# Two fp32r parts instead of three bf16 parts for the rows that the experts gather

## What is computed

```python
xn = rms_norm(x, norm_moe)                       # 256 x 1024
logits = xn @ w_router + b_router
top_val, top_idx = lax.top_k(logits, 4)          # 4 of 32 experts for a token
gates = softmax(top_val)
# for every expert e, with the tokens `tok` that chose it:
hact = clamped_swiglu(xn[tok] @ w_gate_up[e] + b_gate_up[e])   # 1024 -> 2 x 1024 -> 1024
out[tok] += gate * (hact @ w_down[e] + b_down[e])              # 1024 -> 1024
```

## Time and profile before

| | |
|---|---|
| median of 3 runs | 1271.41 us |
| the profiled execution's own time | 1271.19 us |
| its span, first to last instruction | 1269.2 us |
| TensorE (PE) busy | 1187.5 us, 94% of the span |
| VectorE (DVE) busy | 481.7 us, 38% |
| ScalarE (ACT) busy | 250.1 us, 20% |
| mean granted TensorE clock | 0.995 of 2.4 GHz |
| read from device memory | 459.76 MB, 363 GB/s over the span |

### The profile page before, as it was taken

How to read it: one execution, slowest core, us unless ns; L and a number is a source line. 1 busy time by engine, 2 the same in 40 slices (tenths; PEclk the granted TensorE clock), 3 DMA queues, 4 the chain that set the end, 5 groups by cost and what they waited for, 6 DMA issues and landing times.

```text
span 1269.2 us, 18417 instructions
## 1 busy us (share of the span) xinstructions
PE 1187.5 (94%) x7495; PEld 611.8 (48%) x7495; DVE 481.7 (38%) x744; ACT 250.1 (20%) x353; POOL 5.4 (0%) x11
## 2 busy tenths in 40 slices
PE   8999999999799999999999899999999898999996
PEld 7999998998533333333333333333333333333332
DVE  6867867664422322222223222222222222222224
ACT  6338544534410100001000000001000000000002
POOL 0000100000000000000000000000000000000000
PEclk9999999999899999999999999999999999999999
DMA  8525645534999999999999999999999999999995
GB/s 326 195 100 200 253 153 210 186 136 179 400 404 428 428 429 427 428 429 429 429 428 429 427 428 429 429 429 428 429 429 427 429 429 429 428 429 428 428 427 230
DMA packets 36688, 461.28 MB, mean 363 GB/s; under 512 B 4256, under 2 KB 4400, under 8 KB 5552
## 3 DMA queue, kind: packets, MB, share of 16 engines
q1 hardware_dynamic: 36144, 460.16, 86.9%
q0 software_dynamic: 224, 0.54, 0.1%
q10 hardware_dynamic: 288, 0.12, 0.0%
HBM read 459.76 MB, written 1.05 MB: 363 GB/s over the span
## 4 chain that ended last, share of the span: by engine, by line
PE 50%; DMA 47%; ACT 1%; DVE 1%; issue 1%; SPq 0%; DVEq 0%; ACTq 0%
DMA late<-in_w_gate_up 44%; PE ps L1275 21%; PE ps L1146 5%; PE ps L1147 5%; PE ps L1148 5%; DMA raw<-in_w_down 3%; PE ps L1166 2%; PE ps L1165 2%; PE ps L1167 2%; PE ps L1181 2%; PE ps L1326 2%; PE ps L1300 1%; PE ps L1334 1%; DMA raw<-in_dense 1%; PE ps L1234 1%
## 5 line engine op out<-in xcount | busy, mean ns | idle before, releaser
L1275 PE MATMUL ps<-late,s 128*64 128x512 f32 x1128 | 515.9, 600 | 58.0 <-DMA late<-in_w_gate_up 57.0
L1276 PE MATMUL ps<-late,s 128*64 128x512 f32 x1128 | 516.0, 600 | 0.0
L1275 PEld LDWEIGHTS ps<-late,s 128*64 128x64 f32 x1128 | 143.9, 137 | 383.7 <-issue 260.6
L1033 DVE TENSOR_TENSOR res<-res,ps 128x1024 f32<-128x1024 f32 x66 | 80.6, 1221 | 247.7 <-PE ps L1326 247.7
L1146 PE MATMUL ps<-act_hi,whi 128*128 128x256 f32 x576 | 164.1, 285 | 3.8 <-DVE act_lo L693 1.7
L1147 PE MATMUL ps<-act_lo,whi 128*128 128x256 f32 x576 | 163.1, 283 | 0.0
L1148 PE MATMUL ps<-act_hi,wlo 128*128 128x256 f32 x576 | 163.1, 283 | 0.0
L609 ACT ACTIVATE s<-ps 128x512 f32<-128x512 f32 x64 | 34.7, 595 | 561.1 <-PE ps L1276 561.1
L1276 PEld LDWEIGHTS ps<-late,s 128*64 128x64 f32 x1128 | 143.9, 137 | 0.0
L712 DVE TENSOR_TENSOR wlo<-raw,whi 128x2048 fp32r<-128x2048 f32 x47 | 107.4, 2289 | 51.8 <-ACT whi L442 51.7
L1275 PE MATMUL ps<-raw,s 128*64 128x512 f32 x272 | 123.9, 598 | 0.5 <-DMA raw<-in_w_down 0.3
(11 more groups left out here) (178 smaller groups left out, 967.3 us busy)
## 6 DMA issues: line engine op xcount, KB each, us to landing
late<-in_w_gate_up SPq DMA_DIRECT2D x125, 2048.0 KB, 25.5
raw<-in_w_down SPq DMA_DIRECT2D x32, 2048.0 KB, 25.6
raw<-in_dense SPq DMA_DIRECT2D x51, 1024.0 KB, 4.8
late<-in_w_down SPq DMA_DIRECT2D x16, 2048.0 KB, 25.3
s<-in_w_down SPq DMA_DIRECT2D x16, 2048.0 KB, 25.3
raw<-in_w_gate_up SPq DMA_DIRECT2D x2, 2048.0 KB, 9.7
s<-in_w_gate_up SPq DMA_DIRECT2D x1, 2048.0 KB, 12.3
res<-in_x SPq DMA_DIRECT2D x2, 512.0 KB, 4.0
```

The costliest lines, as they stand in the source:

```text
L1033: V.tensor_tensor(res[:, t, :], res[:, t, :], ps[:, OUT_BANK[t]:OUT_BANK[t] + 2, :].rearrange("p b n -> p (b n)"), ALU.add)\
L1275: nc.tensor.matmul(ps[0:SLOTS, bank, :], x_tile, lower, start=start, stop=stop)
L1276: return nc.tensor.matmul(ps[SLOTS:P, bank, :], x_tile, upper, start=start, stop=stop)
```

## The change

The rows are cut into two parts instead of three. ScalarE writes the leading part in fp32r (the rounded value), VectorE subtracts it from the row and writes the remainder in fp32r. `rest_rows_of` and `middle_rows` and their semaphores go; `low_rows` becomes the multiply-and-subtract that `rest_rows_of` was. [...] A gather has 8 x 2 x 2 = 32 products instead of 48. The two parts lie where the three lay (s2 and s3), the one-hot gets a tile of its own.

```diff
-        half = [s[:, :].bitcast(BF16) for s in (s2, s3)]
...
+        xpart = [nc.alloc_sbuf_tensor_at(f"xpart{i}", [P, TT * D], F32R, offset=at)[:, :].rearrange("p (t d) -> p t d", d=D)
+                 for i, at in enumerate((s2_at, s3_at))]
+        onehot = sb("onehot", [P, TT, SLOTS], F32R)
...
-            def middle_rows(t):
-                act.wait_ge(S["part_rest"], t + 1)
-                nc.scalar.activation(xpart[1][:, t, :], rest_rows[:, t, :], ACT.Copy).then_inc(S["part_mid"], 1)
...
-            middle_rows(0)
...
-            middle_rows(1)
...
-            def rest_rows_of(t):
+            def low_rows(t):
                 dve.wait_ge(S["part_hi"], t + 1)
                 dve.wait_ge(S["rstd_done"], t + 1)
-                V.scalar_tensor_tensor(rest_rows[:, t, :], res[:, t, :], rstd[:, 6 + t:7 + t], xpart[0][:, t, :],
-                                       ALU.mult, ALU.subtract).then_inc(S["part_rest"], 1)
-
-            def low_rows(t):
-                dve.wait_ge(S["part_mid"], t + 1)
-                V.tensor_tensor(xpart[2][:, t, :], rest_rows[:, t, :], xpart[1][:, t, :], ALU.subtract)\
+                V.scalar_tensor_tensor(xpart[1][:, t, :], res[:, t, :], rstd[:, 6 + t:7 + t],
+                                       xpart[0][:, t, :].bitcast(F32), ALU.mult, ALU.subtract)\
                     .then_inc(S["part_low"], 1)
...
-            rest_rows_of(0)
             evacuate("xnT", 3, copied(xn_f))
             low_rows(0)
...
-            rest_rows_of(1)
...
-                    for n in range(3):
+                    for n in range(2):
                         for t in range(TT):
                             last = nc.tensor.matmul(ps[:, 5, k * SLOTS:(k + 1) * SLOTS],
                                                     xpart[n][:, t, k * P:(k + 1) * P], onehot[:, t, :],
-                                                    start=n == 0 and t == 0, stop=n == 2 and t == TT - 1)
+                                                    start=n == 0 and t == 0, stop=n == 1 and t == TT - 1)
```

More of the change, by code:

```diff
@@ L176, in build @@
         plain = KT * T
-        s0, s2, s3, s7, s8, s9 = (sb(f"s{i}", [P, plain]) for i in (0, 2, 3, 7, 8, 9))
+        s0 = sb("s0", [P, plain])
+        s2_at = (nc.sbuf_base + 31) // 32 * 32
+        s2 = sb("s2", [P, plain])
+        s3_at = (nc.sbuf_base + 31) // 32 * 32
+        s3 = sb("s3", [P, plain])
+        s7, s8, s9 = (sb(f"s{i}", [P, plain]) for i in (7, 8, 9))
         s15 = sb("s15", [P, 2 * wide])
@@ L259, in build @@
             lam_abs lam_exp pads_zero xr_done pool_done decay_done inner_done mult_done scan_done
-            gelu_arg gelu_sig yb_done m_done lam_done rowmax prob_done part_hi part_rest part_mid part_low
+            gelu_arg gelu_sig yb_done m_done lam_done rowmax prob_done part_hi part_low
             rstd_done router_scaled gmat_zero gate_in gate_exp picked gmat_done bd_placed route_done
@@ L1338, in _ @@
             pe.wait_ge(S["part_hi"], TT)
-            pe.wait_ge(S["part_mid"], TT)
             pe.wait_ge(S["part_low"], TT)
```

## The result

The changed kernel takes **1308.44 us** (median of 4 runs, 1307.68 to 1309.77), the kernel before, run beside it, 1271.38 (4 runs, 1271.1 to 1272.06): a ratio of 1.0295, 95% interval 1.0283 to 1.0308. It is slower by 37 us; the time lies outside the range that was forecast. The profiled execution took 1307.78 us.

What follows compares the result with a forecast made beforehand. The prediction took the memory loads to bound the expert loop, with TensorE having slack. 0 in the loop, +0.8 us at its start and nothing at the end gave 1272.2 us, no change; range 1268.0 to 1278.0.

Steps and rivals of the forecast that it cites:

- the gather's cost: Gather in the loop: 32 products 111 ns apart take 3.44 us from first to last, 2.06 us more than now.
- the slack: Expert loop: TensorE waits 69.4 us in all for loads, so each of 31 gathers may grow by 2.24 us.
- 0 in the loop: Expert loop: the longer gathers, 64 us over 31, are hidden by the loads and add nothing.
- the thin products let the clock fall in every iteration: Rival, loop: 1.2 GHz after each gather costs a few us an expert, beyond the slack; chance 0.08 shared with two passes.
- The start: Before the expert loop: first gather starts about 1.5 us earlier but lasts 7.1 us; first release +0.8 us.
- the two bounds for the release: First buffer release at the loop's start: +2.9 us if the clock stays low throughout, -2.7 us if it never falls.
- The row between: Loop start: clock returns at 346.2, as expert 0 starts at 346.3; release at 350.0, +0.8 us.
- the first rival: Loop gather: products 120 ns apart make TensorE the bound, 3.1 us over the slack, 1275.3 us; chance 0.26.
- Two passes: Rival, loop gather: each product costs two passes, 63 distances, +104 us, about 1376; chance 0.08 shared with the falling clock.
- The faster start: Rival, loop start: the clock does not fall, first release 2.7 us sooner, 1268.7 us; chance 0.16.

Runs made afterwards that it cites:

- e1_split: The changed kernel with each gather of the loop cut into two halves of 16 products, the second behind the first two `down` chunks; 1274.62 us, ratio 1.0028.
- e2_long_bf16: The kernel before with 72 more bf16 products in each gather of the loop, 120 in all; 1272.16 us, ratio 1.0005.
- e8_split_40: The changed kernel with its loop gather in two halves and 40 fp32r products for an expert instead of 32; 1301.96 us, ratio 1.0242.
- e5_warm_after: The changed kernel with 22 and 14 dense bf16 products ahead of the rank products and of the first gather; 1305.54 us, ratio 1.027.
- e6_split_warm: The changed kernel with the loop's gather in two halves and dense bf16 products ahead of the rank products and first gather; 1271.29 us, ratio 1.0004.

## Why the prediction was wrong

**Right: the gather's cost and the slack.** The distance was taken as 111 ns from the four blocks of L1255 and measured 112; the gather was to grow by 2.06 us and grew by 2.18; TensorE's period was to be 28.4 us and is 28.55 at a full clock; the slack of 69.4 us holds all 31 gathers (31 x 2.18 = 67.6 us; e1_split, e2_long_bf16) and little more (e8_split_40). The Trainium skill's rule on the fast weight load ("TensorE: Matmul & The Clock Gate", "Weight-path perf modes — Fast Weight Load (FWL) and DoubleRow") left open whether fp32r counts as FP32. The trace has fp32r go at the pace of the float32 blocks of L1255, 112 ns a block against 0.11 us, where the estimate from the section "LDWEIGHTS (loading the stationary operand)" was 107 ns.

**Wrong: the step that failed is "0 in the loop".** The sum took the clock in the loop as full and put the cost of its fall at nothing. The case stood among the rivals: "the thin products let the clock fall in every iteration" got a share of 0.08 together with another case, no worked-out time, and was left out of the range. A fall came in 21 of 29 periods at 1.68 us, 35 us in all; with the slack spent by the gather itself next to nothing was left to hide it. The argument against it was that no stretch of the loop shows the clock under 1.00 now. That was true and said nothing about the new kernel: in the loop before, every stretch is dense products or the bf16 gather. A row that spoke the other way was used for something else: the clock stayed low through the whole first gather of the kernel before and only came back 4.2 us into expert 0's dense products. It was a hint and no more, since those were bf16 products, and in the loop a long row of them does not let the clock fall (e2_long_bf16). Priced from the prediction's own numbers, the case would have read: expert 0's first products took 5.75 us where 3.65 would do at the full clock, 2.1 us; 31 x 2.1 = 65 us with 5 us of slack left, so up to 60 us, about 1332. The measured 1308 lies below that upper bound.

Which property of the 32 products does it? The runs show that cutting the row of products in two takes the fall away, that the same time of bf16 products 29 ns apart has no fall, and that half of the columns does not change it. The type by itself is not it: the dense stages run fp32r products of 256 columns with TensorE busy throughout and the clock at 1.00 (window 38 to 42 above). No run has bf16 products 112 ns apart, or so long a row of fp32r products with a few more columns, so which property it is stays open. Why some gathers bring no fall stays open too.

The Trainium skill ties the falling clock in the loop of a kernel to gaps in which TensorE waits ("TensorE: Matmul & The Clock Gate", "HAM oscillation — how this bites in real kernels"); this trace has a fall without such a gap, since the clock fell with TensorE busy 4.00 of 4.00 us. Whether the engine pauses inside the 112 ns from one product to the next, the record does not show, because the records of neighbouring products overlap (0.277 us each).

**The start: right in kind, too small.** The forecast had the first gather at 338.3 us, lasting 7.1; it began at 337.69 and lasted 7.00. Of the two bounds for the release, +2.9 us was the right one (+2.28 measured, expert 0 having started 0.6 us sooner than forecast). The row between, "the clock came back 7.9 us after the first product of the gather", failed: at 344 to 348 us the clock is still at 0.50, and the dense products take 0.84 us until about 349.9, 4.2 us after expert 0's start, as before. The 7.00 us of the gather's products did not bring the clock back; it rose among expert 0's. The 4.2 us is no constant either: the rise came 3.6 us after expert 0's start in e5_warm_after (343.62 to 347.2) and 4.8 us after it in e6_split_warm (342.90 to 347.7). The bounds of the forecast held this term.

**The rivals.** TensorE did become the bound, but not by the distance of 120 ns that the first rival named. Two passes did not come: the 32 products are 32 records, 112 ns apart. The faster start did not come: with dense products in the idle time (e5_warm_after) the clock fell in the gather all the same.

## What to carry to other kernels

Price products by the type of their stationary block, not by their number: from first to last start 32 fp32r products take 3.48 us where 48 bf16 products take 1.38, with 64 columns each. Before a row of such products is made longer, price what follows it at half the clock, from the trace's own low stretches, and if it must be long, try dense work in the middle of it (37 us here became 3 to 4). Where a load-ahead runs dry at the start of a loop, look at when the first buffer is released: 2.9 us earlier there gave 2.5 at the end.

## What was not expected of the hardware

The granted clock fell from 2.4 to 1.2 GHz while the record of TensorE has product after product without a gap: its idle time between 383.35 and 1246.47 us is nil (863.12 of 863.12 busy), and the mean clock there is 0.96. A busy TensorE in the profile is no sign of a full clock; the column of the granted clock has to be read by itself. And the distance between the fp32r products did not depend on the moving columns: 32 or 64, both at 112 ns.
